# First turn of the expert layer on experts 0 and 1, the other six ranked: what it does to a one-core transformer kernel

## The reference, cut to what matters

```python
D_MODEL, SEQ, FFN_DIM, N_EXPERTS, TOP_K = 1024, 256, 3584, 8, 2

def moe_ffn(h, w_router, w1, w3, w2):
    logits = (h @ w_router).astype(jnp.float32)
    top_val, top_idx = lax.top_k(logits, TOP_K)
    top_w = jax.nn.softmax(top_val, -1)
    combine = jnp.sum(jax.nn.one_hot(top_idx, N_EXPERTS) * top_w[..., None], -2)
    out = jnp.zeros_like(h)
    for e in range(N_EXPERTS):
        out = out + combine[..., e:e + 1] * swiglu(h, w1[e], w3[e], w2[e])
    return out
```

## Time and profile before

| | before |
|---|---|
| time, median of 3 runs | 2495.08 us (2493.76 to 2495.33) |
| span of the profiled execution, first to last instruction | 2493.3 us |
| time of the runs beyond that span | 1.8 us |
| TensorE busy | 2369.4 us, 95% |
| VectorE, ScalarE busy | 28%, 18% |
| transfers of expert weights | 166 of 2 MB and 4 of 1 MB |
| DMA rate in the expert layer | 387 to 409 GB/s |

### The profile page before, as it was taken

The page is one execution under the profiler, slowest core; times in us unless marked ns, Lnnn a source line. Parts: engine busy times, 40 slices in busy tenths (PEclk is TensorE's granted clock), DMA queues, the critical chain, the costliest instruction groups (busy, mean ns, idle before and its releaser), DMA issues.

```text
span 2493.3 us, 35588 instructions
## 1 busy us (share of the span) xinstructions
PE 2369.4 (95%) x15435; PEld 1396.6 (56%) x15435; DVE 699.8 (28%) x1645; ACT 458.1 (18%) x929; POOL 48.2 (2%) x67
## 2 busy tenths in 40 slices
PE   7999999999999899999999999899999999999998
PEld 5755667856685447777686744544434334343433
DVE  2372465244454514232125543200001000000001
ACT  1322225423212411000032242200000000000000
POOL 3400000000000000000000000000000000000000
PEclk9999999999999999999999999899999999999999
DMA  8953564332322238666323221499999999999997
GB/s 264 209 197 144 197 220 153 127 141 83 90 70 102 73 126 300 243 236 236 127 70 98 81 91 45 164 409 409 401 395 390 404 405 409 409 401 409 409 399 272
DMA packets 210444, 586.52 MB, mean 235 GB/s; under 512 B 14672, under 2 KB 16800, under 8 KB 210288
## 3 DMA queue, kind: packets, MB, share of 16 engines
q1 hardware_dynamic: 206512, 576.93, 62.1%
q0 software_dynamic: 3376, 5.94, 1.3%
q10 hardware_dynamic: 400, 1.36, 0.2%
HBM read 583.14 MB, written 1.06 MB: 234 GB/s over the span
## 4 chain that ended last, share of the span: by engine, by line
PE 82%; DMA 8%; DVE 4%; ACT 3%; issue 1%; DVEq 1%; SPq 1%; ACTq 0%
PE PSB L2772 15%; PE PSA L375 10%; PE PSA L393 10%; PE PSB L2676 8%; DMA RING<-in_w_moe 6%; PE PSA L2806 5%; PE PSB L2781 5%; PE PSA L2654 4%; PE PSA L752 3%; PE PSA L1907 2%; PE PSA L2037 2%; PE PSA L2820 2%; PE PSB L2633 1%; PE PSB L1541 1%; PE PSB L2011 1%
## 5 line engine op out<-in xcount | busy, mean ns | idle before, releaser
L2772 PE MATMUL PSB<-RING,Y 128*64 128x512 f32 x1792 | 402.7, 602 | 29.9 <-DMA RING<-in_w_moe 18.5
L375 PE MATMUL PSA<-RING,HT 128*128 128x512 f32 (+1 forms) x704 | 304.5, 585 | 9.5 <-ACT small L351 3.9
L2772 PEld LDWEIGHTS PSB<-RING,Y 128*64 128x64 f32 x1792 | 135.2, 138 | 269.2 <-issue 266.4
L393 PE MATMUL PSA<-HT,RING 128*128 128x256 f32 x1216 | 276.5, 387 | 6.8 <-DMA RING<-in_w_in_ab 4.4
L393 PEld LDWEIGHTS PSA<-HT,RING 128*128 128x128 f32 x1216 | 233.5, 194 | 41.6 <-issue 10.0
L375 PEld LDWEIGHTS PSA<-RING,HT 128*128 128x128 f32 x704 | 131.4, 192 | 150.3 <-issue 141.0
L2806 PE MATMUL PSA<-RING,ROW 128*64 128x512 f32 x896 | 198.6, 595 | 5.2 <-issue 4.0
L2676 PE MATMUL PSB<-HT,RING 128*128 128x256 f32 x896 | 199.0, 380 | 1.6 <-issue 1.6
L2676 PEld LDWEIGHTS PSB<-HT,RING 128*128 128x128 f32 x896 | 169.2, 190 | 30.7 <-issue 9.0
L2928 DVE TENSOR_TENSOR PROJ<-PROJ,PSB 128x512 f32<-128x512 f32 x28 | 18.2, 685 | 555.1 <-PE PSB L2772 555.1
L2781 PEld LDWEIGHTS PSB<-RING,Y 128*32 128x32 f32 (+1 forms) x3136 | 107.5, 114 | 51.7 <-issue 41.5
(11 more groups left out here) (472 smaller groups left out, 2237.9 us busy)
## 6 DMA issues: line engine op xcount, KB each, us to landing
RING<-in_w_moe SPq DMA_DIRECT2D x166, 2048.0 KB, 19.4
RING<-in_w_ada SPq DMA_DIRECT2D x24, 2048.0 KB, 8.8
RING<-in_w_dense SPq DMA_DIRECT2D x21, 2048.0 KB, 8.8
RING<-in_w_in SPq DMA_DIRECT2D x20, 2048.0 KB, 7.7
RING<-in_w_in_c SPq DMA_DIRECT2D x15, 2048.0 KB, 7.8
RING<-in_w_in_ab SPq DMA_DIRECT2D x10, 2048.0 KB, 19.0
RING<-in_w_out SPq DMA_DIRECT2D x4, 2048.0 KB, 8.0
RING<-in_w_out_ab SPq DMA_DIRECT2D x3, 2048.0 KB, 8.0
```

Source lines behind the costliest of these rows:

```text
L375: mm = pe.matmul(PSA[:, lane[k], 512 * t:512 * t + cols], HT[:, c, P * t:P * t + P], W[:, c, 0:cols], start=(c == 0), stop=(c == KC - 1))
L393: mm = pe.matmul(PSA[:, lane[k], S * j:S * j + S], W[:, c, P * j:P * j + P], HT[:, c, :], start=(c == 0), stop=(c == KC - 1))
L2772: mm = pe.matmul(WIDE_BANKS[i][WIDE * which:WIDE * which + WIDE, :], HTG[:, c, WIDE * which:WIDE * which + WIDE], W[which][:, c - per * kh ...
```

## The change

The first turn always takes experts 0 and 1, so that its transfers need no rank. SP issues them right behind the mixer's own, each as its slot is given up: the order of the four mixer slots is turned (`TURN_SLOT`) so that the slot which is free first is filled first. The other six experts are ranked among themselves; the turns take the 3rd and 4th, the 1st and 6th, the 2nd and 5th. What a turn holds is now given by its place:

- turn 0, `BOTH`: 64 wide and 32 extra columns for each of its experts (the extras as four parts side by side, two for each expert)
- turn 1, `NONE`: 64 wide columns for each, no extra ones
- turn 2, `MOST`: 64 wide for each, 64 extra for `which` = 0, in two parts. This is the body of the hardware loop, which runs once here
- last turn, `SOME`: 64 wide for each, 32 extra for `which` = 0, in four parts

Turns 0 and 1 are written out. In `BOTH` both slots of a pair are given up after the extra matmuls. The gathers for the next turn come in two pieces (in turn 0) or four (in turns 1 and 2), and stand between the down pairs and their halves. The core of the diff:

```diff
-        EXTRA = (P // 2, P // 4)
+        BOTH = Extra(P // 2, 2, tuple((w, j, 64 * w + 32 * j, 32, P + 32 * w) for w in range(2) for j in range(2)))
+        NONE = Extra(0, 0, ())
+        MOST = Extra(P // 2, 2, tuple((0, j, 64 * j, 64, P) for j in range(2)))
+        SOME = Extra(P // 4, 4, tuple((0, j, 32 * j, 32, P) for j in range(4)))
+        CAP_A, CAP_B, CAP_LAST = (96, 64, 128, 128), (96, 64, 64, 64), 96
...
+        next_mixer = (items[-1][1] + 1) % MIX_SLOTS
+        TURN_SLOT = [(next_mixer + j) % MIX_SLOTS for j in range(MIX_SLOTS)] + list(range(MIX_SLOTS, SLOTS))
...
+            pe.matmul(PLACES[:, 0:8], CF[:, C_BEFORE:C_BEFORE + P], chosen[:, 0, :], start=True, stop=True)
...
+            for t in range(NT):
+                dve.scalar_tensor_tensor(e_place[:, t, :], PLACES[:, 8 * t:8 * t + 8], 1.0, chosen[:, t, :], ALU.add, ALU.mult)
+            need(dve, "places")
...
+            dve_select(dve, 0)
+            dve.drain().then_inc(sem("select"), 1)
             dve.max(rank_sorted, rank_key)
...
-        def extra(turn):
-            return EXTRA[0] if isinstance(turn, int) else EXTRA[1]
+        def extra(turn, end=False):
+            if end:
+                return SOME
+            return {0: BOTH, 1: NONE}.get(turn, MOST) if isinstance(turn, int) else MOST
...
+            def release(mm, which, last, wide):
+                if not last:
+                    return
+                if ex is BOTH:
+                    if not wide:
+                        mm.then_inc(sem("item_used"), 1)
+                elif not ex.groups:
+                    mm.then_inc(sem("item_used"), 1)
+                elif wide and which == 1 or not wide:
+                    mm.then_inc(sem("item_used"), 1)
...
-                        for j in range(parts):
-                            mm = pe.matmul(EXTRA_BANK[ec * j:ec * j + ec, i, 0:pw], HTG[:, c, P:P + ec],
-                                           W[0][:, c - per * kh, 512 * i + pw * j:512 * i + pw * j + pw],
+                        for which, j, at, size, col in ex.groups[::-1]:
+                            mm = pe.matmul(EXTRA_BANK[at:at + size, i, 0:pw], HTG[:, c, col:col + size],
+                                           W[which][:, c - per * kh, 512 * i + pw * j:512 * i + pw * j + pw],
...
                     pe_moe_turn(pe, 0)
+                    pe_moe_turn(pe, 1)
                     last = turn_count(pe)
-                    with pe.Fori(1, last) as turn:
+                    with pe.Fori(0, last) as turn:
...
+                if isinstance(turn, int) and turn == 0 and j < SLOTS:
+                    if slot < MIX_SLOTS:
+                        sp.wait_ge(sem("item_used"), last_in[slot] + 1)
+                    else:
+                        sp.wait_ge(sem("scratch_free"), DEPTH)
+                else:
+                    sp.wait_ge(sem("item_used"), upto(PER_TURN, turn, STATIC + j - SLOTS + 1))
+                sp.dma_start(slot_view(j), src).then_inc(sem(f"slot_loaded{slot}"), 16)
...
+            for j in range(PER_TURN):
+                load_item(0, j, [slice(0, 1), slice(1, 2)])
             sp.wait_ge(sem("ranked"), 1)
-            for r in (0, N_EXP - 1):
-                load_rank(r)
-            load_items(0, range(SLOTS))
+            sp.reg_mov(ring[N_EXP - 1], 0)
+            sp.reg_mov(ring[3], 1)
+            for at, rank in zip((0, 1, 2, 4, 5, 6), (2, 0, 1, 3, 5, 4)):
+                sp.reg_mov(ring[at], sp.value_load(rank_i[0:1, rank:rank + 1].bitcast(I32), min_val=0, max_val=N_EXP - 1))
+            load_turn(1, range(PER_TURN))
```

More of the change, by code:

```diff
@@ L1 @@
+from collections import namedtuple
 from contextlib import ExitStack
@@ L2740, in used @@
         def used(turn, what):
-            return PER_TURN * turn + (STATIC + turn_at[what] + 1)
+            return upto(PER_TURN, turn, STATIC + turn_at[what] + 1)
         def pe_moe_turn(pe, turn, end=False):
[L2744 to L2747, removed]
+            ex = extra(turn, end)
+            pw = 512 // ex.parts if ex.groups else 0
+            begun = not (isinstance(turn, int) and turn == 0)
@@ L2768, in first @@
                 per = KC // n
+                order = (0, 1) if ex.groups else (1, 0)
                 for i in range(n):
                     for c in range(per * kh, per * kh + per):
-                        for which in range(2):
+                        last = i == n - 1 and c == per * kh + per - 1
+                        for which in order:
                             mm = pe.matmul(WIDE_BANKS[i][WIDE * which:WIDE * which + WIDE, :],
@@ L2884, in silu_extra @@
             def silu_extra(u):
+                if not ex.groups:
+                    return
                 n = len(STAGES[u])
@@ L2913, in act_moe_turn @@
                 if u == len(STAGES) - 1 and not end:
-                    take_misc(SCATTERS + 1)
-                    take_misc(SCATTERS + 2)
+                    for n in range({BOTH: 2, NONE: 4, MOST: 3}[ex]):
+                        take_misc(SCATTERS + 1 + n)
                 take_extra(u)
-            if not end:
-                take_misc(SCATTERS + 3)
+            if ex is MOST:
+                take_misc(SCATTERS + 4)
         def dve_moe_turn(dve, turn, end=False):
-            pw = 512 * extra(turn) // P
-            begun = not isinstance(turn, int)
+            ex = extra(turn, end)
+            pw = 512 // ex.parts if ex.groups else 0
+            begun = not (isinstance(turn, int) and turn == 0)
             def hidden_wide(u):
-                dve.wait_ge(sem("item_used"), used(turn, (1, "up", (u, len(STAGES[u]) - 1))))
+                wide_done(dve, turn, ex, "up", u)
                 for i, g in enumerate(STAGES[u]):
@@ new lines, in _ @@
+            sp.wait_ge(sem("ranked"), 1)
+            sp.reg_mov(ring[N_EXP - 1], 0)
[3 more added lines that the diff above has]
+            load_turn(1, range(PER_TURN))
+            next_pair()
+            last = turn_count(sp)
+            with sp.Fori(0, last) as turn:
+                load_turn(turn, range(PER_TURN))
+                next_pair()
@@ L3110, in _ @@
+            load_turn(last, range(PER_TURN - 2))
+            e = [sp.snap(ring[r], min_val=0, max_val=N_EXP - 1) for r in (0, N_EXP // 2)]
             for hf in range(2):
```

310 lines of the change are left out of this document (183 added, 127 removed).

## The result

The changed kernel takes 2502.15 us, the median of 8 runs (2499.75 to 2503.10), against 2494.59 us before: a ratio of 1.0029, 95% interval 1.0020 to 1.0039. It is slower, by 5 to 10 us. The forecast was 2496 with a range of 2487 to 2504, and its likeliest case (2492 to 2500, no difference that can be measured) did not come.

The account below looks back on a forecast made before the run. TensorE and DMA were taken as two close limits of the expert layer, ruling turn by turn. Turn gains and losses summed to -0.3 us, plus about 1.2: span 2494.2, time 2496 us, range 2487 to 2504.

Parts of the forecast that it names:

- The chain of four turns: Expert layer: turn 0 ruled by TensorE, turn 1 by DMA, turn 2 and the last turn by TensorE.
- The start of turn 0: TensorE no longer waits for weights and starts at 1603.3 for 1608.12, 0.2 us behind the tokens.
- the tail: From the start of the last turn's second last pair to the end: 28.8 us, left alone by the change.
- the price of a pair in turn 0: Turn 0: 6.87 us wide plus 3.45 extra, 10.32 in all, making the turn 230.8 us.
- its own term: Turn 2 with 64 extra columns: 240.5 us, ruled by TensorE, against 218 of DMA.
- a lump of 1.2: Added to the sum: turn 2's half-clock start (up to 1.5 us) and late transfers in the last turn (0 to 2).
- its term: Last turn up to its second last pair: 184.0 us, ruled by TensorE by 2.5 us over DMA.
- the two limits add up: Slower rival, last turn: seams at turn 2's start and end cost 2 to 3 us each, +5 to +10, 2502; chance 0.17.
- The three signs of being wrong: Turn 2 starting after 2045, turn 2 lasting over 243 us, or the last turn waiting for DMA over 3 us.
- The lead survives: Faster rival: turn 2 isn't TensorE's, so DMA rules to the end; time 2485; chance 0.07.
- Turn 1 falls to half the clock: Slower rival: DMA-fed turn 1 runs at 1.2 GHz throughout, 13.7 us a pair, +71 us, time 2567; chance 0.04.
- four parts that overlap only in part: Slower rival, turn 0: the extra part's 3.45 us becomes 3.9, +9 us; chance 0.05.

Follow-up runs that it names:

- the kernel with the light turn 0: The changed kernel with 32 extra columns in turn 0 for expert 0 alone, none for expert 1: 2480.9 us, ratio 0.9946 against the kernel before.

## Why the prediction held in its mechanism and missed in size

**The chain of four turns stands.** Each turn was ruled by the engine that was named: TensorE, DMA (from its ninth pair on; the eight before it ran at TensorE's pace), TensorE, and TensorE again up to the second last pair, for which DMA came 1.46 us late where the forecast had it 2.5 us early. The start of turn 0 (22.7 for 23.4; of that the 0.2 us taken for the semaphore came as 1600.34 - 1600.19 = 0.15, from the end of ScalarE's last copy), turn 1 (205.0 for 205.6) and the tail (28.6 for 28.8) came as worked out, and with them the claim that most of the lead is lost to seven full slots.

**The step that failed is the price of a pair in turn 0.** "The work per part is that of 256 columns, so I take 3.45" and 6.87 for the wide row beside it. Measured 3.59 and 7.02, 10.61 for 10.32 in the gate and up pairs, somewhat less in the down pairs and at the pieces between, 4.5 us over turn 0. Two runs show that it is the form: 230.6 us with two parts (the forecast of 230.8, for the form it was taken from), 235.3 with four, in either of two orders. The earlier trace rows had it: a wide row beside parts of 32 columns takes 1848.00 - 1841.03 = 6.97 us, beside parts of 64 columns 6.87. I quoted the 7.02 for the old light pairs and took the 6.87 for the new heavy ones, which have parts of 32 columns too. I also gave bounds of 3.45 and 6.9 to the extra part and none to the wide one.

**Turn 2 was 2.1 us longer than its own term** (242.6 for 240.5): 1.7 for the start at half the clock (8.78 for 7.05 us), which I had put at "up to 1.5" inside a lump of 1.2. The earlier trace rows break off inside the first row of turn 2 before; whole it takes 10.05 us, so the trace had shown that such a start can cost 3.0:

```profile
2052.33 10.05 PE L2772 MATMUL PSB<-RING,Y 128*64 128x512 f32 x32 [4.66 <-issue]
```

The run with work in turn 1 shows that part: no wait ahead of turn 2, and 240.9.

**The last turn was 1.8 us over its term**, 1.46 of it the wait for DMA ahead of the second last pair. The prediction let DMA run through this turn at 5.18 us a transfer; reckoned from the same release, (2468.99 - 2283.18 + 3.45 - 8.8) / 34 = 5.31 came. The first and the fourth 21 us of the last turn, and its first 21 us in the kernel with 32 columns in turn 2, where DMA ruled (the last number is DMA's rate):

```profile
2283.00:2304.00 21.00, 21.00 (x201) 9.09 (x198) 3.04 (x3) 1.47 (x3) 0.00 (x0) 1.00 1.01 395
...
2346.00:2367.00 21.00, 21.00 (x230) 9.74 (x220) 1.71 (x3) 2.07 (x4) 0.00 (x0) 1.00 0.99 382
```

```profile
2263.00:2284.00 21.00, 21.00 (x199) 9.06 (x200) 3.04 (x3) 1.47 (x3) 0.00 (x0) 1.00 1.03 409
```

The turn starts with the slots full, and its first pairs, with a scatter each, stand 10.8 us apart (1851.80 - 1841.03 in a turn of the same form before), more than the 10.36 of two transfers. So TensorE holds DMA back at the start, and DMA is late at the end, where the pairs are shorter. Turn 2 and the last turn together took 3.9 us over their terms for 1.2. So, of the 5.7 us between forecast and measurement in the sum (920.0 for 914.3), 4.5 are turn 0's form, 2.7 these two, and -1.5 the start, turn 1 and the tail.

**What was luck.** The range held the 2502 us, but its upper end was set by the added seams, which gave 2.7 us; the 4.5 us of turn 0's form were no part of it. That 2502 is also the number of *the two limits add up* is chance too. The three signs of being wrong stayed silent (turn 2 began at 2040.60 and lasted 242.6 us, and the last turn waited 1.5 us for DMA): none of them looked at turn 0, where most of the miss lies.

**The rivals.** *The lead survives* did not come: turn 2 was TensorE's, with 242.6 us. *Turn 1 falls to half the clock*: a few such restarts are there, and hidden. In the changed kernel TensorE waited 3.1 to 3.2 us ahead of most pairs in the middle of turn 1,

```profile
1916.48 7.09 PE L2873 MATMUL PSA<-RING,ROW 128*64 128x512 f32 x32 [3.16 <-issue]
1926.72 7.09 PE L2831 MATMUL PSB<-RING,Y 128*64 128x512 f32 x32 [3.15 <-issue]
1937.01 7.09 PE L2831 MATMUL PSB<-RING,Y 128*64 128x512 f32 x32 [3.20 <-DMA RING<-in_w_moe]
```

and did so at the full clock (granted clock 1.00 from 1905 to 1983); the wide rows of two later pairs of the turn, and the first of turn 2, took 8.78. In the kernel with the light turn 0 it was six times in turn 1, as here:

```profile
1864.25 8.78 PE L2832 MATMUL PSB<-RING,Y 128*64 128x512 f32 x32 [2.16 <-DMA RING<-in_w_moe]
...
1926.93 9.87 PE L2832 MATMUL PSB<-RING,Y 128*64 128x512 f32 x32 [4.35 <-DMA RING<-in_w_moe]
```

9.87 us is still under DMA's 10.36 a pair, and the turn took DMA's 217.5. The Trainium skill's rule ("TensorE: Matmul & The Clock Gate", HAM oscillation), that each such group can restart at the half rate, is borne out in part: there are rows of 8.78 us behind waits of 2 us, but 2 and 6 of them in turn 1 where the prediction reckoned with 21, and rows of 7.09 us behind waits of 3.2. In the changed kernel a restart costs time only at the start of turn 2, 1.7 us, since TensorE rules from there on. *The two limits add up* and *four parts that overlap only in part* each came in small, 2.7 and 4.5 us, the first without its sign: the last turn's only wait for DMA comes at its twentieth pair, not before the tenth. I had treated them as alternatives (0.17 and 0.05) where they were two terms of one sum, both with one sign. That is why a sum of 2496 with a chance of 0.60 was too sure: most of what I had left open could only lengthen it.

## What to carry to other kernels

Where two limits lie within a few per cent, a lead in one of them is worth only what the next stage can use: the same early transfers were worth 9 to 11 us ahead of a stage ruled by TensorE and 23 us ahead of one ruled by DMA, so lighten the stage behind the lead first. Work taken out of a stage that waits anyway is worth little (36 us of it were worth 1.6 here), and work added to a stage that TensorE rules lengthens the chain (11 us here for turn 2's wider extra part). Price a new instruction form by the row whose shape it shares, its neighbour rows included, and add small one-sided unknowns up instead of giving each a chance of its own.

## What the runs showed of the hardware

A wide row ahead of 32-column parts takes 7.02 us from its start to the next row's, ahead of 64-column parts 6.87 to 6.89, and four parts of 32 columns by 256 take 3.59 us where two of 64 by 256 take 3.45: 0.26 to 0.29 us a gate or up pair with no wait on any other engine, in both orders of the parts that were run. Waits of 3.2 us ahead of most pairs left the granted clock at 2.4 GHz in one stretch (1905 to 1983 in the changed kernel), and a wait of 2.2 us in another brought a row that starts at 1.2 GHz (8.78 us for 7.09). Such a row costs some 1.7 us in most cases and 2.4 to 3.0 in others (9.52 and 10.08 in the second run without early transfers, 10.07 with 32 columns in turns 0 and 1); it was hidden where waits for DMA followed (six of them in a turn of 217.5 us at DMA's pace). The part ahead of the experts, the same instructions in all kernels, moved by up to 7.5 us between profiles, and by as much between three of one kernel, while the sum of the stages behind it repeated within 0.5 us in those three.
